# Two transformer blocks on one core: all sixteen up-projection pairs in the seven-product form, value projection in 512 columns

## The reference

```python
# first block
h = rmsnorm(x, pre_mlp_norm)
u = square(relu(h @ w_up))            # w_up 1024 x 4096
x = x + rmsnorm(u @ w_down, post_mlp_norm)
# second block
h = x @ w_in                          # holds pooled part, q, k, v (512 columns each) and forget logits
...
x = layer_norm(ALPHA * x + mix, ln1_g, ln1_b)
hid = square(relu(x @ w_mlp1))        # 1024 x 4096
x = layer_norm(ALPHA * x + hid @ w_mlp2, ln2_g, ln2_b)
```

## Time and profile before

| | |
|---|---|
| median of three runs | 2557.14 us |
| profiled execution | 2556.62 us |
| its span | 2554.8 us |
| mean granted clock | 0.999 |
| PE busy | 2510.1 us (98%) |
| DVE busy | 1474.2 us (58%) |
| ACT busy | 1056.8 us (41%) |
| DMA | 347.59 MB, mean 136 GB/s |

### The profile page before, as it was taken

One profiled execution on the slowest core, in us unless ns is written; L12 is line 12 of the kernel. 1 busy time (PEld: TensorE's weight loads), 2 busy tenths in 40 slices (PEclk: granted clock), 3 DMA queues, 4 the chain that ended last, 5 costly groups with the idle time before them and its releaser, 6 DMA issues.

```text
span 2554.8 us, 30682 instructions
## 1 busy us (share of the span) xinstructions
PE 2510.1 (98%) x12072; PEld 2080.0 (81%) x12072; DVE 1474.2 (58%) x2153; ACT 1056.8 (41%) x1698; POOL 189.9 (7%) x173
## 2 busy tenths in 40 slices
PE   7999999999999999999999999999999999999998
PEld 6777888888888788888888887876788888888886
DVE  4345223223533777766664754358768676576668
ACT  4344322222322544444434542358526444444433
POOL 0000000000020300000000110145111000000000
PEclk9999999999999999999999999999999999999999
DMA  4121211111422426547875542101313364588554
GB/s 166 66 75 66 75 42 40 36 34 59 156 83 74 149 77 220 188 158 262 307 252 188 181 158 65 34 20 41 112 53 128 142 228 140 178 320 326 186 190 168
DMA packets 129679, 347.59 MB, mean 136 GB/s; under 512 B 13152, under 2 KB 13408, under 8 KB 129408
## 3 DMA queue, kind: packets, MB, share of 16 engines
q1 hardware_dynamic: 129536, 345.63, 38.7%
HBM read 256.91 MB, written 85.52 MB: 134 GB/s over the span
## 4 chain that ended last, share of the span: by engine, by line
PE 90%; DVE 5%; issue 2%; ACT 1%; DMA 1%; POOL 1%; SPq 0%; DVEq 0%; ACTq 0%; POOLq 0%
PE bank L643 28%; PE bank L645 28%; PE bank L644 28%; DVE PAl L2407 1%; DVE st L2402 1%; PE bank L704 1%; POOL accX L2588 1%; PE bank L754 1%; PE bank L821 1%; PE bank L1070 1%; PE bank L831 0%; PE bank L825 0%; PE bank L789 0%; ACT PAh L1680 0%; DVE wlo L1740 0%
## 5 line engine op out<-in xcount | busy, mean ns | idle before, releaser
L1740 DVE TENSOR_TENSOR wlo<-raw,whi 128x1024 fp32r<-128x1024 f32 x102 | 125.2, 1234 | 253.3 <-ACT whi L1143 252.7
L643 PE MATMUL bank<-hhi,whi 128*128 128x512 f32 x608 | 249.2, 410 | 1.7 <-DVE hlo L1765 1.7
L645 PE MATMUL bank<-hhi,wlo 128*128 128x512 f32 x608 | 238.8, 393 | 0.0
L644 PE MATMUL bank<-hlo,whi 128*128 128x512 f32 x608 | 238.7, 393 | 0.0
L1143 ACT ACTIVATE whi<-raw 128x1024 fp32r<-128x1024 f32 x102 | 106.6, 1054 | 102.2 <-PE bank L645 86.2
L643 PEld LDWEIGHTS bank<-hhi,whi 128*128 128x128 f32 x608 | 115.0, 189 | 29.4 <-issue 6.7
L645 PEld LDWEIGHTS bank<-hhi,wlo 128*128 128x128 f32 x608 | 114.8, 189 | 25.3
L644 PEld LDWEIGHTS bank<-hlo,whi 128*128 128x128 f32 x608 | 115.1, 189 | 22.5
L1448 ACT ACTIVATE r<-r 128x512 f32<-128x512 f32 x78 | 49.0, 629 | 134.1 <-DVE r L2225 97.6
L643 PE MATMUL bank<-yhi,whi 128*128 128x512 f32 x192 | 74.9, 390 | 0.0
L645 PE MATMUL bank<-yhi,wlo 128*128 128x512 f32 x192 | 74.7, 389 | 0.0
(11 more groups left out here) (477 smaller groups left out, 7183.3 us busy)
## 6 DMA issues: line engine op xcount, KB each, us to landing
ra<-ud_d SPq DMA_DIRECT2D x112, 512.0 KB, 4.5
raw<-wp_d SPq DMA_DIRECT2D x102, 512.0 KB, 3.6
rbh<-wp_d SPq DMA_DIRECT2D x64, 512.0 KB, 5.3
rawp<-wp_d SPq DMA_DIRECT2D x26, 1024.0 KB, 5.8
ud_d<-us SPq DMA_DIRECT2D x104, 256.0 KB, 5.6
rbw<-wp_d SPq DMA_DIRECT2D x48, 512.0 KB, 3.6
ud_d<-f SPq DMA_DIRECT2D x76, 256.0 KB, 2.0
rbx<-wp_d SPq DMA_DIRECT2D x32, 512.0 KB, 7.6
```

The source lines that it names most:

```text
L643: e.matmul(P, sh, mh, start=first, stop=False, skip_group_check=more)
L644: e.matmul(P, sh, ml, start=False, stop=False, skip_group_check=more)
L645: return e.matmul(P, sl, mh, start=False, stop=last, skip_group_check=more)
L1740: e.tensor_tensor(out=wlo[n % SLOTS][:, :], in0=raw[n % RAWS][:, :], in1=whi[n % SLOTS][:, :].bitcast(F32), op=ALU.subtract).then_inc(*up( ...
```

## The change

The six plain tiles are gone, and all 32 column tiles form 16 pairs. The two products of the tile's own weights, A11 x B11 (`first`) and A12 x B21 (`second`), are made for all 16 pairs in `up_order`, from the same weight pieces and slots as the plain tiles before. After `first`, ACT copies the bank to one of two buffers and SP stores it in DRAM (`fd`). `second` adds into the same bank, and ACT makes Relu and Square of it, which SP stores too (`ud[A21]`). The order of `up_order` is new and the same on all engines: step `rest` or `side`, make `first` of the next pair (two of them in step 0), make `second` of the pair before. The feed is held meanwhile.

In the pair loop five products remain. `xu` brings the two kept results back from DRAM, one pair ahead (`fetch_first`). The sums of weights have three buffers instead of two. The order of DVE, ACT and SP in a pair is new. The extra sums for plain tiles and their traffic are gone. The value projection is made in 512 columns, 8 token tiles of 8 x 3 matmuls (`token_wide`, `wide_product`), and its evacuation takes eight heads at once.

```diff
-NPIECES = 102
-CAT = 88
-NSTD = 6
-NSTART = 5
-NPAIRS = 16 - NSTD // 2
+NPIECES = 122
+CAT = 98
+NPAIRS = 16
-def up_order(feed, half_product, name, specs, rest, side, lead=False):
-
-    feature_major_start(feed, half_product, name, specs[:NSTART], rest, side, lead, 4)
-    for m in range(NSTART, NSTD):
-        for _ in feature_major(feed, half_product, name, m, specs[m]):
+def up_order(feed, name, first, second, rest, side):
+
+    ns = []
+    feed.held = True
+    for j in range(NPAIRS):
+        if next(rest, "end") == "end":
             next(side, None)
+        for p in (0, 1) if j == 0 else range(j + 1, min(j + 2, NPAIRS)):
+            ns.append(feed.piece("F", name, 2 * p))
+            feed.ahead(min(feed.cur + 2, ns[0] + SLOTS) if j < 4 else feed.cur + 2)
+            first(ns[p], p)
+        for p in range(max(j - 1, 0), j if j < NPAIRS - 1 else NPAIRS):
+            second(ns[p], p)
+            feed.done(ns[p])
+    feed.held = False
+    run(rest)
+    run(side)
...
# PE, one pair
-                e.wait_ge(*ok("a1l", tag, p))
-                product("a", 0, a1h[b], a1l[b], 0, *part(0, 0))
                 e.wait_ge(*ok("a1l", tag, "s24", p))
                 product("b", 0, s24h[b], s24l[b], 0, *total(1))
-                product("a", 1, a1h[b], a1l[b], 512, *part(4, 0))
                 e.wait_ge(*ok("a1l", tag, "s13", p))
+                product("c", 0, s13h[b], s13l[b], 0, *total(0))
                 product("b", 1, s13h[b], s13l[b], 512, *total(2))
-                product("c", 0, s13h[b], s13l[b], 0, *total(0))
+                product("c", 1, s24h[b], s24l[b], 512, ...)
                 e.wait_ge(*ok("a1l", tag, "a22", p))
                 product("b", 2, a22h[b], a22l[b], 0, *total(3))
-                product("c", 1, s24h[b], s24l[b], 512, *part(4, 512))
...
# DVE, one pair (new order)
+                if p:
+                    block_21(p - 1)
+                if more:
+                    weight_sums(p + 1)
+                    weights_a22(p + 1)
+                ...                                   # r12 = b0 + p1
+                if p:
+                    sums_of_u(p - 1)
+                ...                                   # r22 = c0 + p1
+                if more:
+                    weights_s24(p + 1)
+                else:
+                    u_low(0)
+                    u_low(1)
+                ...                                   # r22 += b1
+                if more:
+                    weights_s13(p + 1)
+                else:
+                    w_sum(0)
+                ...                                   # r12 += c1
+                if not more:
+                    w_low(0)
...
# DVE, after the loop
+            block_21(last)
             w_sum(1)
-            finish_12(last)
             w_low(1)
             sums_of_u(last)
```

More of the change, by code:

```diff
@@ L278, in token_major, with token_wide @@
         yield
+def token_wide(feed, wide_product, name, spec):
+    ns = [feed.piece("V", name, k) for k in range(4)]
+    for t in range(NT):
+        wide_product(ns, t, spec)
+        if t == 7:
+            for n in ns:
+                feed.done(n)
+        yield
 def rows_group(feed, row_product, name, ks, spec, after=None, between=nothing):
@@ L1401, in mlp @@
         def mlp(tag, up_name, acc, rest, norm, early, late):
-            first = feed.cur + NSTD
-            feed.cap = first
+            end = feed.cur + NPAIRS
+            feed.cap = end
             last = NPAIRS - 1
[L1406 to L1424, removed]
-                e.wait_ge(*ok("rawp", tag, p))
[L1426 to L1432, removed]
+            def first(n, p):
+                e.wait_ge(*ok("full", "sa" + tag, p, 0))
+                if p > 1:
+                    e.wait_ge(*ok("uo", tag, "p1", p - 2))
+                e.activation(p1s[p % 2][:, :], bank_of("sa" + tag, p, 0)[:, :], ACT.Copy).then_inc(*free("sa" + tag, p, 0))
@@ new lines, in second @@
+            def second(n, p):
+                e.wait_ge(*ok("full", "sa" + tag, p, 1))
+                if p:
+                    e.wait_ge(*ok("usq", tag, "11", p - 1))
+                e.activation(r11[:, :], bank_of("sa" + tag, p, 1)[:, :], ACT.Relu).then_inc(*free("sa" + tag, p, 1))
+                e.wait_ge(*ok("free", "sa" + tag, p, 1))
+                if p > 1:
+                    e.wait_ge(*ok("uo", tag, "11", p - 2))
+                e.activation(f11[p % 2][:, :], r11[:, :], ACT.Square).then_inc(*up("usq", tag, "11", p))
@@ L1454, in squared @@
                 e.activation(f[:, :], r[:, :], ACT.Square).then_inc(*up("usq", tag, name, p))
[L1456 to L1459, removed]
-                e.wait_ge(*(ok("us", tag, S3, p - 2) if p > 1 else ok("uo", tag, "std", 8 + p)))
-                e.activation(f11[p % 2][:, :], r11[:, :], ACT.Square).then_inc(*up("usq", tag, "11", p))
             def u_high(s):
@@ L1549, in sums_of_h @@
                 yield
-                e.wait_ge(*ok("a1l", tag, "a22", 0))
+                yield
                 sum_high(3)
                 yield
-            side = sums_of_h()
-            up_order(feed, half_product, up_name, [std_product(m) for m in range(NSTD)], rest, side, lead=True)
-            run(side)
+            up_order(feed, up_name, first, second, rest, sums_of_h())
             for p in range(NPAIRS):
@@ L1560, in mlp @@
             w_high(1)
-            squared("12", last, r12[last % 2], r12[last % 2])
             for i in range(STEPS_DOWN):
@@ L2789, in mlp @@
         def mlp(tag, up_name, rest, i, norm, early, late):
-            first = feed.cur + NSTD
-            feed.cap = first - RAWS
+            end = feed.cur + NPAIRS
+            feed.cap = end - RAWS
             last = NPAIRS - 1
@@ L2875, in second_pair @@
                 yield
-            up_order(feed, half_product, up_name, [std_out(m) for m in range(NSTD)], then_pair(), second_pair(), lead=True)
+            up_order(feed, up_name, first, second, then_pair(), first_pairs())
             for p in range(NPAIRS):
                 if p:
-                    pair_out("22", p - 1)
                     pair_out("21", p - 1)
@@ L2970, in sync_program @@
         feed.cap = CAT
-        for vh in range(2):
-            run(token_major(feed, nothing, "v_2", 256 * vh, None))
+        run(token_wide(feed, nothing, "v_2", None))
         def duplicates(t):
```

339 lines of the change are left out of this document (157 added, 182 removed), and 2 rows, old and new, of the table CHAINS.

## The result

The changed kernel takes 2572.88 us (median of four runs, 2571.67 to 2574.08) beside 2557.01 for the kernel before: ratio 1.0062, 95% interval 1.0045 to 1.008, so 0.6% slower. The forecast was 2566 us, within 2550 to 2582. The profiled execution took 2574.08, 1.2 above the median; its span is 2572.3, 17.5 more than before and 8.7 more than the 2563.6 forecast for it; the mean granted clock is 0.992 instead of 0.999.

What follows compares the result with a forecast made beforehand. PE, busy 98% of the span, was taken to bound the kernel. 2554.8 - 16.3 - 2.0 + 9.5 + 10.2 + 6.9 + 0.5 = 2563.6 us of span; plus 1.8 and 0.5, 2566 us, range 2550 to 2582.

Steps and rivals of the forecast that it cites:

- Matmuls and value projection: Both MLPs lose 72 matmuls at 0.227 us, 16.3 us less; the value projection in 512 columns gains net 2.0 us.
- First start: Start of the first MLP: new PE waits of 4.4, 3.5, 0.4 and 3.9 us, less the old 2.7: +9.5 us.
- third-piece wait: In each start PE waits for the third weight split's low part: 3.5 us in the first MLP, 2.15 in the second.
- Second start: Start of the second MLP: new PE waits of 3.1, 2.15 and 4.9 us: +10.2 us, bounds 5 and 14.
- the sixth split's: Second MLP's start: split behind four sums from 1948.6, ending at 1958.9 against PE at 1954.2: a wait of 4.9 us.
- Pair loop: 13.6 us per pair with DVE at 11.1; 0.5 us added for both MLPs, bounds 0 and 10.
- The margin of 0.15 us: In each pair, DVE's chain releases the bank for PE's fourth product with 0.15 us to spare.
- Seam: Passage from pair loop to down projection: three delays, 3.4 us per MLP, +6.9 in all, bounds 0 and 12.
- The bank: Last pair: bank b is free at 11.4 us, so the fifth product waits 0.8 us.
- the start of the down projection: The first weight difference and its high and low part end at 15.2 us, so the down projection starts 0.85 late.
- step 3: In the down projection, its transfers are issued behind the last, later sum of u; it comes 1.75 us late.
- rival (4): Granted clock falls after the new idle stretches: up to 12 us, more likely one or two stalls, 2569 to 2572; chance 0.15.

Runs made afterwards that it cites:

- filler: The changed kernel with 68 unread matmuls of 512 columns put into PE's waits at both starts: 2568.44 us, 1.0048.
- the kernel with the addition in the chain: The changed kernel with one more 128x512 DVE addition per pair, ahead of the addition that frees the bank of PE's fourth product: 2586.27 us, 1.0117.
- the addition off the chain: The changed kernel with one more 128x512 DVE operation per pair, behind the addition that frees the bank of b: 2572.04 us, 1.0059.
- the first experiment (sixth split): The changed kernel with only the feed's limit changed, so the sixth weight piece may be split before step 4 of the start: 2560.23 us, 1.0014.
- the third (seam): The changed kernel with last-pair fetches ahead of block 21's store, b's bank released earlier and later transfers ahead of the last four stores: 2563.95 us, 1.0027.
- both together: The changed kernel with the earlier sixth weight split and the reordered passage to the down projection in one: 2551.21 us, 0.9982.
- the fifth kernel: The changed kernel with the start reordered on all engines and the passage to the down projection reordered too: 2551.16 us, 0.9978.

## Why the forecast held, and where it was short

The direction and its reason were right: the waits of two starts cost more than 72 matmuls give (26.8 us against 16.3). The time was 6.9 us short by the medians, 8.7 by the spans.

- **Matmuls and value projection** (-16.3, -2.0). As forecast; the -16.3 is worked out from the step and not measured by itself, and the stages sum up with it.
- **First start** (+9.5, measured +12.7). The waits, forecast 4.4, 3.5, 0.4, 3.9, are 4.37, 0.77, 0.25 and 3.55. The third-piece wait is short only since PE came late to it, at the low clock; at full clock it is 3.18 (filler). The rest of the 12.7 is slow matmuls, some 5.3 us by 0.9 for the transposes, 8 times 0.2 and 14 times 0.2, and restarts.
- **Second start** (+10.2, measured +14.1). Waits forecast 3.1, 2.15 and 4.9, found 3.09, 0.21 (1.81 at full clock) and 6.45. The step that failed is the sixth split's: "1948.6 + 4 x 2.28", which put the first sum 0.7 us later than before. The store before it was indeed issued 0.6 later within the stage (22.3 after the last projection matmuls, 21.8 before), but took until 4.6 us after its issue to release DVE, against 2.7 before, so that the first sum came 2.5 later within the stage, and PE's wait was 1.55 longer than forecast. That this is the step is shown by the kernel with the addition in the chain, whose start has the same program: there the store, issued at 1958.93, released DVE after 2.74, and PE waited 4.56, near the 4.9. With the addition off the chain, again the same start, it was 4.38, and PE waited 6.2. What makes the store slow stays open. The DMA engines are busier while it runs than in the kernel before, but they are as busy in the run where it is quick (rows below). Of its neighbours, the store 1.9 us ahead of it and the one 1.0 behind stand at the same places there; a load and a store further ahead were issued 0.7 and 1.0 us earlier. No run moved these alone.

The sums in the kernel after and in the one with the addition in the chain, and PE's wait in the latter:

```profile
1957.80 2.29 DVE L2051 TENSOR_TENSOR T1hf<-zlo 128x2048 f32<-128x2048 f32 x1 [4.78 <-DMA xd_d<-accX]
...
1961.67 2.29 DVE L2051 TENSOR_TENSOR T1hf<-zlo 128x2048 f32<-128x2048 f32 x1 [2.88 <-DMA xd_d<-accX]
...
1972.00 0.80 PE L654 MATMUL bank<-zhi,whi 128*128 128x512 f32 x1 [4.56 <-DVE wlo L1746]
```

Windows from the store's issue to the release: the kernel before, the kernel after (with the stretch ahead of the issue), and with the addition in the chain:

```profile
1945.20:1947.90 2.70, 2.70 (x13) 2.24 (x12) 1.23 (x1) 2.02 (x3) 0.00 (x0) 1.00 0.48 194
...
1950.00:1953.20 3.20, 3.20 (x20) 2.76 (x19) 1.29 (x2) 3.11 (x6) 0.00 (x0) 1.00 1.01 373
1953.20:1957.80 4.60, 4.60 (x22) 3.82 (x21) 0.00 (x0) 1.83 (x3) 0.00 (x0) 1.00 0.82 324
...
1958.90:1961.70 2.80, 2.80 (x14) 2.33 (x13) 0.03 (x1) 0.60 (x2) 0.00 (x0) 1.00 0.85 334
```

- **Pair loop** (+0.5, measured 0). The margin of 0.15 us was read rightly (0.17 in the trace after); 0.7 us more in the chain costs 0.52 per pair.
- **Seam** (3.4 per MLP, measured 5.1 and 4.2 with the pair loop's part). The bank costs 0.52 and 0.84 (forecast 0.8), the start of the down projection 2.23 and 1.56 with a restart (forecast 0.85), step 3 0.20 and 1.75 (forecast 1.75), less in the first MLP as the down projection began later. The first weight difference started behind 1.04 us of idle time on DVE, where the forecast had none; that it waited for its transfers is the likely reason, since in the kernel with the seam reordered they are issued earlier and the wait is gone. In the first MLP one wait more came last, which the forecast doesn't name: the profile puts the 2.23 down to block 21 of the last pair (line 2185), which ends 0.6 us behind the low part of the weights. It frees a bank, and the down projection opens its banks by fixed numbers. Nine matmuls behind the 2.23 are slow, the first and the last of them in part, some 1.6 us.

The rows of this, in order of time: in the first MLP PE at the bank, the low part and block 21 on DVE, and PE at the down projection; in the second MLP PE at the down projection and at step 3.

```profile
1192.06 0.47 PE L654 MATMUL bank<-T4h,a22h 128*128 128x512 f32 x1 [0.52 <-DVE r L2216]
...
1195.30 1.23 DVE L2168 TENSOR_TENSOR uw0bl<-Tw,uw0bh 128x1024 fp32r<-128x1024 f32 x1 [0.52 <-ACT uw0bh L1512]
1196.45 0.68 DVE L2185 TENSOR_TENSOR r<-bank,xu 128x512 f32<-128x512 f32 x1
...
1197.27 0.47 PE L654 MATMUL bank<-uw0bh,uw0ah 128*128 128x512 f32 x1 [2.23 <-DVE r L2185]
...
2256.01 0.50 PE L654 MATMUL bank<-uw0bh,uw0ah 128*128 128x512 f32 x1 [1.56 <-DVE uw0bl L2168]
...
2274.38 0.50 PE L654 MATMUL bank<-uw0bh,uw0ah 128*128 128x512 f32 x1 [1.75 <-DVE uw0bl L2168]
```

- **The clock** was rival (4), which had, with a chance of 0.15, another outcome than the forecast. It is the step that was missing in the sum: not another way in which it could go, but what comes on top of waits of this size. The net price is 4.4 us in the starts by the filler run's median and some 1.6 at the seam by the trace, 6.0 of the 6.9. By the spans it is 4.9 and 1.6, and the sixth split of the second start adds 1.55 (6.45 for 4.9), together 8.1 of the 8.7. Rival (4) named four stalls of 3.5 us or more. Three of them had the low clock behind them; the fourth, at the third piece, had shrunk to 0.77. To these came the 3.09, which it didn't name, and the 2.23 at the seam. Its size (one or two stalls of 3 us, 2569 to 2572) was near, but in part by luck: five stretches were slow, and the waits at the third piece gave some 4 us back.

## What to carry to other kernels

When plain work that hides a stage's tail is cut into smaller units, look at who issues what behind whom: here the new order cost 36 us in all, most of it by a limit of the feed, transposes ahead of products, a split behind a sum and a fetch behind a store; the work saved 18, and better orders took back 29. A wait of PE of several us has a price of its own, here up to 3 us in what follows. It belongs in the same term of the sum, with nothing as its lower end, as it needn't come, and as a later wait can take it back. For a chain on a less busy engine, write out its order with its steps: a margin of 0.15 us on an engine 80% busy was found again as 0.17.

## What the runs showed of the hardware

- Whether the clock falls behind a wait, and for how long, isn't told by the wait alone. The same 3.09 us in the second start was followed by eight transposes in 1.93 us in the changed kernel, and in 1.94, 1.32 and 1.06 in the kernels of the first experiment (sixth split), of the third (seam), and of both together (at full clock elsewhere: 1.03). The rows of the last two kernels:

```profile
1930.23 1.32 PE L728 MATMUL bank<-ident,lx 128*128 128x128 f32 x8 [3.09 <-DVE lx L2470]
```

```profile
1923.38 1.06 PE L728 MATMUL bank<-ident,lx 128*128 128x128 f32 x8 [3.09 <-DVE lx L2470]
```

- A wait of 2.23 us at the first seam, with 0.52 of idle 5 us ahead, was followed by nine slow matmuls (granted clock 0.70, the row below). Those of 1.56 and 1.75 in the second MLP weren't followed by any, nor was the 2.29 of the kernel before; the 1.87 of the fifth kernel was, by eight, behind six at full speed. So a forecast of this price needs a range from 0 to the 2.9 us seen.

```profile
1197.30:1203.00 5.70, 5.70 (x18) 4.57 (x19) 4.49 (x6) 2.07 (x3) 0.00 (x0) 0.70 0.99 390
```

- The granted clock also reads below 1 within some waits (0.83 in 870.40 to 875.00), and 0.50 in the windows above whose matmuls are all 0.43 us apart; at the kernel's own beginning it read 1.00 beside the same steps. For products of float32r the step between starts is the safer sign. It isn't for plain float32: the products of `pd` and `pw` beside attention (512 columns, four from 1697.50 in the kernel after) are 0.43 apart at a granted clock of 1.00, and a float32r one of 512 columns between them (1699.50) takes a step of 0.24.
- A store of 512 KB, the last of the token tiles, released its waiter after 2.7 us in the kernel before and in the one with the addition in the chain, and after 4.6 in the changed kernel, whose start is the same program as the latter's.
